# Thirteen of 31 convolution taps formed by ScalarE, four folding instructions moved earlier, and new interleaving tables for the second layer

## The chip, the cores and the metric

The kernel runs on one core of one Trainium2 chip. The metric is the device time of one execution in microseconds (us), the median of several executions. One core has five engines with a queue each: TensorE (PE, matrix products into the PSUM accumulators; PEld is its weight load), VectorE (DVE), ScalarE (ACT), GpSimd (POOL) and SyncE (SP, transfers only). Instructions of one queue run in order, and queues meet through semaphores.

## The reference

A two-layer trunk over 272 tokens (16 learned ones and 256 frames) of width 1024, float32. Each layer does

```
z = rms(h) @ w_in                       # 1024 -> attention | RWKV | convolution columns
h = h + concat[attention(z), rwkv7(z), conv(z)] @ w_out
h = h + peer(rms(h))                    # product-key experts, 128 x 128 of them
```

The attention has 8 query heads over 2 key/value heads, windows of chunks of 64 tokens, a sink for each head. The RWKV-7 part is a recurrence over tokens in 4 heads of 64. The part that the change is about is the convolution, on 256 channels:

```
u = z[..., :256] * sigmoid(z[..., 256:])
u = depthwise_conv(u, conv_w, 31 taps, causal) + conv_b     # u[t] = sum_k conv_w[k] * u[t - 30 + k]
conv = silu(layernorm(u) * ln_g + ln_b)
```

and the end of the RWKV part, `((y_normalised * gn_g + gn_b) + bonus) * g`, which the kernel computes as `y_normalised * (gn_g * g) + (bonus + gn_b) * g`.

## The kernel before, in words

Everything is written out by hand, one program for each engine, with semaphores between them. Data lie with the channels on the 128 partitions and the tokens along the free axis, so a 256-channel array is two halves (j = 0, 1) of 128 x 272.

A layer has these stages. (1) The projection with w_in, 18 weight tiles of 128 x 1024 from memory; ScalarE rounds each tile to w_hi (`high`, L691), GpSimd forms the rest w_lo = w - w_hi (`low`, L609), and TensorE makes three products for each chunk of 128. The input is split likewise into x_hi and x_lo; these two arrays ("projection input fields") are free once the projection is over. (2) The mixers. (3) The projection with w_out, 8 tiles, of the same kind. (4) A norm and the PEER experts, most of the layer's time.

In the mixer stage the recurrence is solved in chunks of 64 tokens, five chunks. VectorE forms decayed arrays (up to L1630, `rh`), TensorE makes the products `gram`, VectorE masks them (L1637), and a triangular inverse is built by doubling in `LEVELS`: in each level b = 0..4 and for each half j, TensorE makes a product, ScalarE copies it out of PSUM (`xm`, L866), TensorE makes two more, VectorE subtracts them (L1664, L1667). `cms` (L1493) prepares the next level's mask. Then come products W and U (copied by L871 on ScalarE and by L1676 on VectorE), the steps from chunk to chunk (`carry`, L1683, L1689, L1694), the output yT (L878), the group norm (L1704 to L1711) and its end (L1717, L1718), which uses `gg` and `bonus`. These two were prepared at L1671 and L1673, two instructions for each half, that stand between the last level and L1676; they are called the folding.

Two other strands are laid between these instructions. The attention runs for each group of query tokens through: scores on TensorE, their combination with the distance (L1523, VectorE), maximum and subtraction (L1529 to L1533), exponentials (L763, L768, ScalarE), normalising (L1541 to L1543), transposes on TensorE (L1059) with copies (L778), outputs on TensorE with a copy (L783). At its beginning the queries' and keys' norms are made: ScalarE's square root (L666, which needs a load of its function table), then VectorE L1501 to L1509, then the first scores. Layer 0 has more groups (the 16 learned tokens too). The convolution's own norm (`conv_norm`: L1552 to L1567 on VectorE, a root and a sigmoid on ScalarE at L666 and L797) is the last strand.

Each engine has a `Beside` that decides where the strands' pieces go: the main sequence calls it at numbered points, and tables give the point for each piece (`ATT_PE`, `ATT_ACT`, `ATT_DVE`, `CONV_...`, one row for each layer). A smaller number is an earlier place in the engine's queue.

The convolution itself runs on GpSimd alone, from the end of its part of the projection. It forms u (L621) with 30 zero columns ahead of it, and then for each of 31 taps k: two TENSOR_SCALAR instructions (L625, one for each half, u shifted by k times the weight column, into `ctmp`) and one TENSOR_TENSOR (L633, `cacc = cacc + ctmp`; none for k = 0). Behind the last tap come the first `low` instructions of w_out (three before they must wait), then the rest of them. What waits for the convolution is the product of its sums on TensorE, near the end of the mixer stage.

## Time and profile before

| | |
|---|---|
| time, median of 3 executions | 2044.98 us (2039.74 to 2053.9) |
| the profiled execution | 2045.54 us |
| its span, first to last instruction | 2043.7 us |
| TensorE busy in the span | 1957.8 us (96%) |
| VectorE busy | 1451.6 us (71%) |
| GpSimd busy | 1222.8 us (60%) |
| ScalarE busy | 969.3 us (47%) |
| mixer stage of layer 0 | about 80 to 193.6 us of the span |
| mixer stage of layer 1 | about 1107.5 to 1215.2 us |

In the rows below a timeline row is: start, duration, engine, line of the source, operation, out<-in with partitions x elements and type, xN for N instructions put together, and in square brackets how long the engine was idle just before and which engine's instruction ended the wait. "arena" is one large array in the core's memory that holds most of the mixers' data; "ps" is PSUM. A windows row gives, for a stretch of the span, the length, the busy time and count of instructions of each engine, TensorE's granted clock as a share of full speed, and the transfers' share and rate. L971 is the helper through which nearly all matrix products go.

### The profile page before, as it was taken

The numbers are of one execution on the slowest core, as the hardware profiler recorded it, in microseconds if no ns is written. First come the engines' busy times: TensorE is split into PE (matmuls) and PEld (weight loads), VectorE is DVE, ScalarE is ACT, GpSimd is POOL, SyncE is SP. The second block draws the span as 40 slices with busy tenths as digits, with TensorE's granted clock in tenths as the row PEclk, the third lists the DMA queues.
The fourth block names the chain that finished last, engine by engine and source line by source line (L and its number), as shares of the span: only waits on it lengthen the run. The fifth ranks groups of instructions, "written<-read, shape, count | busy, mean of one in ns | idle before, by whom it ended". The sixth has DMA issues, their size and how long they took to land.

```text
span 2043.7 us, 43730 instructions
## 1 busy us (share of the span) xinstructions
PE 1957.8 (96%) x16544; PEld 1874.7 (92%) x16544; DVE 1451.6 (71%) x2792; ACT 969.3 (47%) x1663; POOL 1222.8 (60%) x667
## 2 busy tenths in 40 slices
PE   9977999999999999999999879999999999999999
PEld 9866999999999999999989769999999999999998
DVE  3776249975777788788747852599347777887886
ACT  5524455544333455555455234555543334555553
POOL 5893669997666633233048946799966665332330
PEclk9988999999999999999999889999999999999999
DMA  5300445554444599888643004555544446998994
GB/s 197 105 2 18 143 169 194 178 184 156 151 147 144 210 329 315 288 316 310 243 150 124 2 22 154 177 185 195 185 147 152 144 146 246 335 322 302 326 332 149
DMA packets 106382, 388.18 MB, mean 190 GB/s; under 512 B 11808, under 2 KB 12064, under 8 KB 106016
## 3 DMA queue, kind: packets, MB, share of 16 engines
q1 hardware_dynamic: 87840, 319.61, 45.3%
q0 software_dynamic: 18432, 67.12, 9.4%
q8 instruction: 68, 1.11, 0.2%
q14 instruction: 42, 0.34, 0.1%
HBM read 385.63 MB, written 1.05 MB: 189 GB/s over the span
## 4 chain that ended last, share of the span: by engine, by line
PE 61%; POOL 22%; issue 13%; DVE 2%; ACT 1%; DMA 0%; POOLq 0%; ACTq 0%
PE ps L971 61%; POOL w_lo L609 14%; POOL arena L633 4%; POOL arena L625 3%; DMA arena<-ur_c,sel 0%; DVE x L1478 0%; ACT w_hi L691 0%; DVE x_lo L1471 0%; DVE onehots_j L1466 0%; DVE h L1908 0%; POOL arena L621 0%; DVE sel L1794 0%; DVE h L1907 0%; ACT L843 0%; ACT L666 0%
## 5 line engine op out<-in xcount | busy, mean ns | idle before, releaser
L971 PE MATMUL ps<-x_hi,w_hi 128*128 128x240 f32 (+5 forms) x4768 | 1432.2, 324 | 28.9 <-DVE x_lo L1471 12.4
L971 PE MATMUL ps<-x_hi,w_lo 128*128 128x240 f32 (+3 forms) x4768 | 1308.4, 274 | 0.0
L609 POOL TENSOR_TENSOR w_lo<-w,w_hi 128x1024 fp32r<-128x1024 f32 x346 | 869.8, 2531 | 387.1 <-ACT w_hi L691 386.8
L971 PEld LDWEIGHTS ps<-x_hi,w_hi 128*128 128x128 f32 x4768 | 906.3, 190 | 83.9 <-POOL w_lo L609 12.7
L971 PEld LDWEIGHTS ps<-x_hi,w_lo 128*128 128x128 f32 x4768 | 911.1, 191 | 0.0
L691 ACT CAST w_hi<-w 128x1024 fp32r<-128x1024 f32 x596 | 623.9, 1047 | 345.7 <-PE ps L971 177.1
L971 PE MATMUL ps<-x_lo,w_hi 128*128 128x240 f32 (+3 forms) x2720 | 758.6, 279 | 0.0
L971 PEld LDWEIGHTS ps<-x_lo,w_hi 128*128 128x128 f32 x2720 | 520.8, 191 | 0.2
L1865 DVE TENSOR_TENSOR w_lo<-w,w_hi 128x1024 fp32r<-128x1024 f32 x250 | 305.9, 1224 | 113.3 <-ACT w_hi L691 112.6
L971 PE MATMUL ps<-arena 64*64 64x64 f32 (+11 forms) x2580 | 167.4, 266 | 28.0 <-DVE arena L1509 7.9
L971 PEld LDWEIGHTS ps<-arena 64*64 64x64 f32 (+7 forms) x2580 | 146.2, 164 | 48.8 <-issue 16.1
L936 ACT ACTIVATE arena<-ps 128x224 f32<-128x224 f32 (+29 forms) x116 | 31.2, 269 | 264.8 <-PE ps L971 264.8
L918 ACT ACTIVATE arena<-ps 128x240 f32 (+3 forms) x140 | 51.1, 365 | 169.7 <-PE ps L971 169.4
L971 PE MATMUL ps<-onehots_i,onehots_j 128*128 128x128 f32 x928 | 124.0, 277 | 4.8 <-DVE onehots_i L1821 4.8
L971 PEld LDWEIGHTS ps<-onehots_i,onehots_j 128*128 128x128 f32 x928 | 113.5, 193 | 5.2 <-DVE onehots_i L1821 5.2
L644 POOL DMA_INDIRECT x<-v_c,sel x27 | 44.3, 1642 | 102.3 <-DVE arena L1890 56.3
L1830 DVE TENSOR_TENSOR arena<-arena,ps 128x4 f32<-128x4 f32 (+56 forms) x114 | 31.4, 276 | 99.6 <-ACT ps L938 99.6
L1859 DVE TENSOR_TENSOR x_hi<-arena,x_hi 128x240 fp32r<-128x240 f32 (+1 forms) x256 | 100.6, 394 | 0.9 <-ACT x_hi L945 0.9
L945 ACT CAST x_hi<-arena 128x240 fp32r (+3 forms) x256 | 96.9, 380 | 2.4 <-DVE arena L1840 2.4
L1749 DVE MAX8 arena<-arena 128x8 f32<-128x128 f32 (+1 forms) x102 | 25.2, 321 | 96.7 <-ACT arena L908 96.4
L633 POOL TENSOR_TENSOR arena<-arena 128x544 f32<-128x544 f32 x60 | 81.3, 1355 | 5.0
L1814 DVE TENSOR_TENSOR ps<-ps,sel 128x512 f32<-128x512 f32 x116 | 80.1, 691 | 0.0
(198 smaller groups left out, 1655.0 us busy)
## 6 DMA issues: line engine op xcount, KB each, us to landing
w<-u_c SPq DMA_DIRECT2D x256, 512.0 KB, 3.3
w<-v_c SPq DMA_DIRECT2D x256, 512.0 KB, 5.1
w<-w_c SPq DMA_DIRECT2D x84, 512.0 KB, 3.3
arena<-keys_c SPq DMA_DIRECT2D x2, 1024.0 KB, 5.8
arena<-mix_c SPq DMA_DIRECT2D x2, 964.0 KB, 8.4
h<-h SPq DMA_DIRECT2D x2, 544.0 KB, 4.4
out<-x SPq DMA_DIRECT2D x4, 256.0 KB, 2.2
arena<-lora_c SPq DMA_DIRECT2D x2, 256.0 KB, 9.2
```

The costliest lines, as they stand in the source:

```text
L609: g.tensor_tensor(low_of(l, n, wlo_t), low_of(l, n, wraw_t), high_of(l, n).bitcast(F32), ALU.subtract).then_inc(s_lo, 1)
L625: ins = g.tensor_scalar(dst[:, j, :], cu[:, j, k:k + T], vcol(l, "conv_w", j * CONV_K + k), vcol(l, "conv_b", j) if k == 0 else 0.0, ALU.m ...
L633: ins = g.tensor_tensor(cacc[:, :, :], cacc[:, :, :], ctmp[:, :, :], ALU.add)
L644: g.indirect_dma_start(rows[n % ROWS], None, tables[k // SLOTS], bass.IndirectOffsetOnAxis(g_idx[:, k % SLOTS:k % SLOTS + 1], 0)).then_inc ...
L691: nc.scalar.copy(high_of(l, n), low_of(l, n, wraw_t)).then_inc(s_hi, 1)
L918: nc.scalar.activation(hid[l][:, bass.ds(UN * it + i, 1), :].squeeze(1), ps[:, 1 + i % UB, 0:L.nd], ACT.Gelu_apprx_tanh).then_inc(s_gelu, 1)
L945: nc.scalar.copy(act_pair(L, i)[0], hid[l][:, bass.ds(UN * it + i, 1), :].squeeze(1)).then_inc(s_ah, 1)
L971: return nc.tensor.matmul(out_, lhsT, rhs, start=start, stop=stop, skip_group_check=True)
L1814: v.tensor_tensor(eq, iota_ps, bc(sel[:, 1, g:g + OHT], 2, P), ALU.is_equal).then_inc(s_dl, 1)
L1830: v.tensor_tensor(row, row, ps[:, 1 + (L.split + k) % UB, 0:OHT * k], ALU.mult).then_inc(s_hm, 1)
L1859: v.tensor_tensor(al_, hid[l][:, i, :], ah.bitcast(F32), ALU.subtract).then_inc(s_act, 1)
L1865: v.tensor_tensor(low_of(l, n, wlo_t), low_of(l, n, wraw_t), high_of(l, n).bitcast(F32), ALU.subtract).then_inc(s_lv, 1)
```

## The change

Three things.

1. The taps k = 5, 7, 9, ... 27 and 28, thirteen of them, are formed by ScalarE: two ACTIVATE instructions each (Identity with the weight column as scale; `conv_taps`, L828 of the new code), into eight slots of two halves, four in the memory of x_hi (called `taps`) and four in that of x_lo (`x`). GpSimd only adds such a tap (L640 of the new code) after a wait for it. The other 18 taps stay as they were. From the ninth on, ScalarE waits until GpSimd has added the tap whose slot it takes. The instruction that writes x_hi for w_out waits for the whole convolution.
2. The folding stands right behind `rh`, ahead of the masks.
3. The tables of layer 1 are new, for TensorE, ScalarE and VectorE; those of layer 0 are as before, but for `TAP_ACT`, which is new and serves both layers.

```diff
 CONV_PE = ((51, 52,),
-           (51, 52,))
+           (49, 52,))
 CONV_DVE = ((37, 38, 38, 38,),
-            (37, 38, 38, 38,))
+            (36, 38, 38, 38,))
-          (6, 7, 10, 29, 31, 33, 40, 42, 42, 47, 49, 50, 53,))
+          (6, 7, 9, 18, 19, 20, 27, 29, 35, 48, 51, 53, 53,))
+ACT_TAPS = tuple(range(5, 31, 2))[:-1] + (28,)
+TAP_ACT = (0,) * 7 + (1, 1, 2, 2, 3, 4)
+TAP_SLOTS = 8
...
                 for k in range(CONV_K):
+                    if k in ACT_TAPS:
+                        made += 1
+                        pool.wait_ge(s_tap, len(ACT_TAPS) * l + made)
+                        ins = g.tensor_tensor(cacc[:, :, :], cacc[:, :, :], tap(made - 1), ALU.add)
+                        ins.then_inc(s_tapc, 1)
+                        pool.wait_ge(s_tapc, len(ACT_TAPS) * l + made)
+                        continue
...
+            def conv_taps(l):
+
+                act.wait_ge(s_cu, l + 1)
+                for i, k in enumerate(ACT_TAPS):
+                    if i >= TAP_SLOTS:
+                        act.wait_ge(s_tapc, len(ACT_TAPS) * l + i - TAP_SLOTS + 1)
+                    for j in range(2):
+                        ins = nc.scalar.activation(tap(i)[:, j, :], cu[:, j, k:k + T], ACT.Identity,
+                                                   scale=vcol(l, "conv_w", j * CONV_K + k))
+                    ins.then_inc(s_tap, 1)
+                    yield
...
-                beside = Beside((conv_norm(l), CONV_ACT[l]), (attention(l), ATT_ACT[l]))
+                beside = Beside((conv_taps(l), TAP_ACT), (conv_norm(l), CONV_ACT[l]), (attention(l), ATT_ACT[l]))
...
                 act.wait_ge(s_toc, A0[l + 1])
+                act.wait_ge(s_conv, l + 1)
                 x_high(l, 1, cat, L.t0, range(4))
...
                 ask_pe(v.tensor_tensor(rh[:, :, w], dall[:, :, w], r_, ALU.mult))
+                for j in range(2):
+                    link(v.scalar_tensor_tensor(bonus[:, j, :], bonus[:, j, :], vcol(l, "gn_b", j), gg[:, j, :],
+                                                ALU.add, ALU.mult))
+                    link(v.tensor_scalar(gg[:, j, :], gg[:, j, :], vcol(l, "gn_g", j), None, ALU.mult))
...
-                for j in range(2):
-                    link(v.scalar_tensor_tensor(bonus[:, j, :], bonus[:, j, :], vcol(l, "gn_b", j), gg[:, j, :],
-                                                ALU.add, ALU.mult))
-                    link(v.tensor_scalar(gg[:, j, :], gg[:, j, :], vcol(l, "gn_g", j), None, ALU.mult))
                 k, (c0, cn, bank) = [(k, x) for k, x in enumerate(WU) if x[2] == WU_DVE][0]
```

ScalarE's queue in layer 0, from the last copies of the projection's output over the five `vkb` copies to the square root of the attention's norms, before:

```order
L733 COPY arena<-ps 128x272
L853 COPY arena<-ps 128x512 x5
L666 ACT_TABLE_LOAD
L666 ACTIVATE arena<-ps,res 128x272
L666 ACTIVATE arena<-ps,res 128x24
```

and in the changed kernel, whose line numbers are larger by about 21 to 34:

```order
L754 COPY arena<-ps 128x272
L886 COPY arena<-ps 128x512 x5
L828 ACTIVATE taps<-arena,vecs 128x272 x8
L828 ACTIVATE x<-arena,vecs 128x272 x6
L687 ACT_TABLE_LOAD
L687 ACTIVATE arena<-ps,res 128x272
L687 ACTIVATE arena<-ps,res 128x24
```

Seven of the thirteen taps stand between the copies and the table load of the root; the place is the same in layer 1. The other six follow between the copies of the first levels. In layer 1 these places of ScalarE's queue are, before, from the two copies ahead of the levels (L857, L859):

```order
L857 COPY arena<-ps 128x4x128
L859 COPY arena<-ps 128x128
L866 COPY arena<-ps 128x320 x4
L763 ACT_TABLE_LOAD
L763 ACTIVATE arena<-arena 128x144 x4
L768 ACTIVATE arena<-arena 128x4
L866 COPY arena<-ps 128x320 x2
```

and now, where L899 is the copy of a level (`xm`), L828 a tap's half and L784 the exponentials:

```order
L892 COPY arena<-ps 128x128
L899 COPY arena<-ps 128x320
L828 ACTIVATE x<-arena,vecs 128x272 x2
L828 ACTIVATE taps<-arena,vecs 128x272 x2
L899 COPY arena<-ps 128x320
L828 ACTIVATE taps<-arena,vecs 128x272 x4
L784 ACT_TABLE_LOAD
L784 ACTIVATE arena<-arena 128x144 x4
L789 ACTIVATE arena<-arena 128x4
L784 ACTIVATE arena<-arena 128x144 x2
L899 COPY arena<-ps 128x320
L828 ACTIVATE taps<-arena,vecs 128x272 x2
```

Before, the four copies of levels 0 and 1 had nothing between them; now a table load, six exponentials and eight halves of taps stand among the first three of them, and two more halves behind the third.

VectorE's queue in layer 1, at the end of the levels, before (L1523 is the last attention group's scores, L1671 and L1673 the folding, L1683 the first carry):

```order
L1667 TENSOR_TENSOR arena<-arena,ps 128x320
L1541 TENSOR_TENSOR arena<-arena 128x4
L1542 RECIPROCAL arena<-arena 128x4
L1543 TENSOR_TENSOR arena<-arena 128x576
L1671 SCALAR_TENSOR_TENSOR arena<-arena,vecs 128x272
L1673 TENSOR_SCALAR arena<-arena,vecs 128x272
...
L1676 TENSOR_SCALAR arena<-ps 128x512
L1523 SCALAR_TENSOR_TENSOR arena<-arena,ps 128x208 x4
L1529 TENSOR_REDUCE arena<-arena 128x4
...
L1543 TENSOR_TENSOR arena<-arena 128x832
L1683 TENSOR_TENSOR arena<-ps,arena 128x128
```

and now (L1557 scores, L1705 the last updates, L1563 to L1577 the attention's chain, L1710 the copy, L1717 the carry):

```order
L1705 TENSOR_TENSOR arena<-arena,ps 128x320
L1557 SCALAR_TENSOR_TENSOR arena<-arena,ps 128x208 x4
L1705 TENSOR_TENSOR arena<-arena,ps 128x320 x2
L1563 TENSOR_REDUCE arena<-arena 128x4
...
L1577 TENSOR_TENSOR arena<-arena 128x832
L1710 TENSOR_SCALAR arena<-ps 128x512
L1717 TENSOR_TENSOR arena<-ps,arena 128x128
L1723 TENSOR_TENSOR arena<-ps,arena 128x384
```

The last group's scores moved ahead of the last two updates, and the folding is gone from here; nothing of the attention stands between the copy L1710 and the first carry any more.

## Rows read from the trace of the kernel before

**Rows 1.** The page's engine totals, then busy time by stretch (columns as explained above).
```profile
PE 1957.8 (96%) x16544; PEld 1874.7 (92%) x16544; DVE 1451.6 (71%) x2792; ACT 969.3 (47%) x1663; POOL 1222.8 (60%) x667
...
80.00:193.60 113.60, 85.66 (x1419) 74.60 (x1419) 81.06 (x151) 39.77 (x114) 79.30 (x91) 0.84 0.02 6
...
1107.50:1215.20 107.70, 82.82 (x1380) 71.67 (x1379) 69.61 (x127) 35.73 (x93) 78.90 (x91) 0.81 0.02 7
1215.20:1241.00 25.80, 25.74 (x197) 25.23 (x197) 8.62 (x20) 11.51 (x19) 19.84 (x8) 0.92 0.44 144
```

**Rows 2.** Timeline of GpSimd: a tap of layer 0, first w_lo behind it (both layers).
```profile
152.03 0.96 POOL L625 TENSOR_SCALAR arena<-arena,vecs 128x272 f32<-128x272 f32 x2
153.08 1.33 POOL L633 TENSOR_TENSOR arena<-arena 128x544 f32<-128x544 f32 x1
...
156.84 7.73 POOL L609 TENSOR_TENSOR w_lo<-w,w_hi 128x1024 fp32r<-128x1024 f32 x3
...
1184.70 6.97 POOL L609 TENSOR_TENSOR w_lo<-w,w_hi 128x1024 fp32r<-128x1024 f32 x3
```

**Rows 3.** Timeline of ScalarE in layer 0: a scaled pair, the table load, the root.
```profile
41.00 0.98 ACT L828 ACTIVATE arena<-arena,vecs 128x272 f32<-128x272 f32 x2
...
85.55 1.28 ACT L666 ACT_TABLE_LOAD   x1
91.28 0.66 ACT L666 ACTIVATE arena<-ps,res 128x272 f32<-128x272 f32 x2 [4.45 <-PE ps L971]
```

**Rows 4.** Timeline of TensorE: the first scores, behind the root and VectorE's norms.
```profile
97.10 0.39 PE L971 MATMUL ps<-arena 64*16 64x16 f32 x8 [4.11 <-DVE arena L1509]
```

**Rows 5.** Timeline of VectorE in layer 0: mask, attention chain, folding, next scores.
```profile
87.02 0.69 DVE L1637 TENSOR_TENSOR arena<-ps,arena 128x512 f32<-128x512 f32 x1 [9.22 <-PE ps L971]
...
153.66 0.76 DVE L1530 TENSOR_TENSOR arena<-arena 128x4 f32<-128x4 f32 x1
...
155.79 1.71 DVE L1543 TENSOR_TENSOR arena<-arena 128x576 f32<-128x576 f32 x1
157.43 2.58 DVE L1671 SCALAR_TENSOR_TENSOR arena<-arena,vecs 128x272 f32<-128x272 f32 x1
...
165.31 0.69 DVE L1676 TENSOR_SCALAR arena<-ps 128x512 f32<-128x512 f32 x1
167.33 0.90 DVE L1523 SCALAR_TENSOR_TENSOR arena<-arena,ps 128x208 f32<-128x208 f32 x2 [1.33 <-PE ps L971]
```

**Rows 6.** Timeline of TensorE in layer 0 over the same stretch.
```profile
157.65 1.94 PE L1059 MATMUL ps<-res,arena 128*128 128x128 f32 x8 [4.24 <-DVE arena L1543]
159.52 11.88 PE L971 MATMUL ps<-arena 64*64 64x128 f32 x216
```

**Rows 7.** Timeline of VectorE and then of TensorE in layer 1.
```profile
1150.16 0.48 DVE L1667 TENSOR_TENSOR arena<-arena,ps 128x320 f32<-128x320 f32 x1
...
1150.96 0.76 DVE L1543 TENSOR_TENSOR arena<-arena 128x576 f32<-128x576 f32 x1
...
1170.15 0.47 DVE L1667 TENSOR_TENSOR arena<-arena,ps 128x320 f32<-128x320 f32 x1
...
1186.23 1.83 DVE L1523 SCALAR_TENSOR_TENSOR arena<-arena,ps 128x208 f32<-128x208 f32 x4 [8.60 <-PE ps L971]
...
1189.42 2.28 DVE L1531 TENSOR_TENSOR arena<-arena,vecs 128x4 f32<-128x4 f32 x1
...
1193.36 0.28 DVE L1683 TENSOR_TENSOR arena<-ps,arena 128x128 f32<-128x128 f32 x1
...
1201.21 0.92 DVE L1704 SCALAR_TENSOR_TENSOR arena<-ps,arena 128x272 f32<-128x272 f32 x2 [2.48 <-PE ps L971]
...
1179.09 3.23 PE L971 MATMUL ps<-arena 128*64 128x128 f32 x16 [1.41 <-ACT arena L778]
1183.09 9.15 PE L971 MATMUL ps<-arena 64*128 64x208 f32 x176 [0.76 <-ACT arena L783]
...
1215.17 0.55 PE L971 MATMUL ps<-x_hi,w_hi 128*128 128x256 f32 x1 [4.60 <-DVE x_lo L1471]
```

More of the change, by code:

```diff
@@ L94 @@
 CONV_DVE = ((37, 38, 38, 38,),
-            (37, 38, 38, 38,))
+            (36, 38, 38, 38,))
 ATT_PE = ((6, 7, 9, 16, 17, 18, 25, 26, 27, 33, 35, 38, 40, 42, 43, 47, 49, 50, 53,),
-          (6, 7, 10, 29, 31, 33, 40, 42, 42, 47, 49, 50, 53,))
+          (6, 7, 9, 18, 19, 20, 27, 29, 35, 48, 51, 53, 53,))
 ATT_ACT = ((0, 0, 0, 2, 2, 2, 3, 5, 6, 6, 6, 8, 8, 8, 9, 10, 12, 12, 12, 13, 13, 13, 13, 16, 18,),
-           (0, 4, 4, 6, 8, 8, 8, 12, 12, 13, 13, 13, 13, 14, 14, 16, 18,))
+           (0, 2, 2, 2, 3, 4, 4, 6, 6, 6, 8, 10, 13, 13, 16, 18, 18,))
 ATT_DVE = ((0, 0, 1, 2, 6, 8, 8, 13, 15, 15, 21, 21, 21, 30, 31, 31, 32, 32, 32, 34,),
-           (0, 0, 2, 2, 7, 12, 16, 26, 29, 31, 32, 32, 32, 34,))
+           (0, 0, 2, 2, 4, 8, 10, 15, 16, 16, 26, 31, 31, 33,))
 class Layer:
@@ L260, in trunk @@
         h_t = sb("h", DC * T)
-        xh_t = sb("x_hi", DC * T, F32R)
+        xr_t, xh_t = twice("taps", "x_hi", DC * T)
         xn_t, xl_t = twice("x", "x_lo", DC * T)
@@ L275, in trunk @@
         tok = lambda t: t[:, :].rearrange("p (c t) -> p c t", c=DC)
-        xn, xh, xl = tok(xn_t), tok(xh_t), tok(xl_t)
+        xn, xh, xl, xr = tok(xn_t), tok(xh_t), tok(xl_t), tok(xr_t)
         vecs = vec_t[:, :].rearrange("p (l n) -> p l n", l=DEPTH)
@@ L300, in trunk, with tap @@
         tables = ur_c, v_c.rearrange("l i p d -> (l i p) d")
+        def tap(i):
+            c = i % TAP_SLOTS * 2
+            return (xr if c < DC else xn)[:, c % DC:c % DC + 2, :]
         def res(name):
@@ L493, in trunk @@
         s_conv = sem("conv_done")
+        s_cu = sem("conv_input_ready")
+        s_tap = sem("conv_tap_ready")
+        s_tapc = sem("conv_tap_added")
         s_cm = sem("conv_sums_in_psum")
@@ L620, in _ @@
                 link(g.memset(cu[:, :, 0:CPAD], 0.0))
-                link(g.tensor_tensor(cu[:, :, CPAD:CPAD + T], z[:, ZCU:ZCU + 2, 1:T + 1], cacc[:, :, :], ALU.mult))
+                g.tensor_tensor(cu[:, :, CPAD:CPAD + T], z[:, ZCU:ZCU + 2, 1:T + 1], cacc[:, :, :],
+                                ALU.mult).then_inc(s_cu, 1)
+                pool.wait_ge(s_cu, l + 1)
+                made = 0
                 for k in range(CONV_K):
+                    if k in ACT_TAPS:
[5 more added lines that the diff above has]
+                        continue
                     for j in range(2):
```

## The prediction

> **What bounds the kernel now.** I read the page's engine totals first. TensorE is busy in 1957.8 of 2043.7 us, VectorE in 71%, GpSimd in 60%, ScalarE in 47% [rows 1]. TensorE is thus the bound nearly everywhere, and there is only 2043.7 − 1957.8 = 86 us in which it stands still. The busy time by stretch says where: 113.6 − 85.7 = 27.9 us in the mixer stage of layer 0 and 107.7 − 82.8 = 24.9 us in that of layer 1, 53 of the 86 [rows 1]. Behind layer 1's mixers TensorE is busy for 25.74 of 25.80 us. The change touches only the two mixer stages, and in them it adds no matrix product and removes none, so what it can change is these 53 us of waiting and the time in which TensorE runs at less than full clock: the granted share is 0.84 and 0.81 there and still 0.92 in the 25.8 us behind [rows 1].
>
> Then the timelines, one engine after another. A tap takes GpSimd 1.05 us from its first TENSOR_SCALAR to the add and 1.33 + 0.1 for the add, 2.48 in all [rows 2]. The last tap ends at 156.8 and 1184.7, where the first three w_lo begin, while the projection with w_out begins at 193.6 and 1215.2. So the convolution isn't late: the group norm's L1704 starts only at 1201.2 [rows 7], and the product of the convolution's sums stands beside it in the program. GpSimd is a bound of nothing here, and **a shorter convolution gives nothing by itself**. What it can give is less interference: VectorE's instructions with two inputs in the core's memory take longer beside GpSimd. One on 128x4 elements took 2.28 us in layer 1 [rows 7] and another 0.76 in layer 0 and the folding's first 2.58 [rows 5].
>
> **The change part by part.**
>
> *Taps on GpSimd.* Thirteen taps lose their pair: 13 x 1.05 = 13.6 us for each layer. The convolution ends at about 144 and 1172, and the three w_lo of 7.0 to 7.7 us [rows 2] begin there. This costs or gives TensorE nothing directly.
>
> *Denser adds.* The two-input adds now follow each other closer: two in 1.05 + 1.43 + 1.43 = 3.9 us in place of 4.96 in the stretch with alternate taps. If each VectorE instruction with two inputs has to wait for a running GpSimd instruction to end, its mean wait with the old pattern is (2 x 0.48² + 1.33²)/2/2.48 = 0.45 us and with the new (2 x 0.48² + 2 x 1.33²)/2/3.9 = 0.51, an eighth more. There are some ten such instructions on the path up to the levels, so +0.5 to +1.0 us for each layer.
>
> *Seven taps ahead of the root.* This is the part on the path. Their 14 instructions stand between the last `vkb` copy, which ends at 85.5 (the table load begins at 85.55), and the table load of 1.28 us. The same form, 128x272 with a column for scale, took 0.98 us for two, with about 0.41 us from one to the next [rows 3]. So 14 x 0.415 + 0.15 = 5.96 us: ScalarE is through at 91.4 or 91.5, the load ends at 92.7, and the root starts there, where it started at 91.28. The 4.45 us of idle time ahead of the root [rows 3] cover the rest. Delay: **+1.44 us in each layer**. It isn't hidden by what follows: VectorE makes the keys behind the root, and TensorE waited 4.11 us for their last copy, L1509 [rows 4]. The ends for the range: 0 if the pitch is 0.31 us (14 x 0.1 us less), +2.7 if each tap's half takes 0.5 us.
>
> The trace shows no engine idle behind a table load: the next instruction starts at once where its input is there. The Trainium skill, ScalarE: Activation LUTs, "What ACT_TABLE_LOAD costs", has a drain of 1.38 us besides the 1.28 us of each switch; by it the root would be later by 2.8 us and not 1.44 in each layer, and the gain below smaller by 2.8 us in sum. Rows here can't show it, because this root waited anyway.
>
> *The other six taps.* They stand between the level copies. In layer 0 the copies wait for TensorE longer than a tap's 0.83 us, so 0. In layer 1 see below.
>
> *The folding.* In layer 0 it ran from 157.43 to 165.3 on VectorE, 7.9 us, but TensorE had 11.88 us of products from 159.5 on [rows 6], and the next scores then still waited 1.33 us for TensorE [rows 5]. Taking it away there gives 0. At its new place VectorE was idle for 9.22 us ahead of the mask [rows 5]; even with the 7.9 us that they took they fit: 0. Layer 1's queue is the same up to there, so 0 too.
>
> *Layer 0 in sum.* +1.44 for the root, +0.5 for denser adds. Against it stands one gain: the attention chain from 153.66 to 157.5 that TensorE waited 4.24 us for [rows 6] falls behind the end of the convolution, yet beside the w_lo instructions only until about 152. Its normalising took 1.71 us [rows 5] where one of the same shape took 0.76 in layer 1 [rows 7]; that is 0.95, and the first 128x4 instruction with 0.76 us and those behind it hold about as much again, so −2.0 us. **Layer 0: 0 us**, ends −2 and +3.
>
> *Layer 1's tables.* Before, VectorE's last update ended at 1170.6 (call this T) and the first carry started at 1193.36, 22.7 us later [rows 7]. Between them lay the folding, the outputs of one group on TensorE (3.23 us at 1179.09), the scores of the last (from 1183.09; VectorE waited 8.60 us for them) and the whole chain of that group on VectorE, 7.1 us from 1186.23 to 1193.36 with one instruction of 2.28. Now nothing of that stands there but one chain and its normalising (about 5 us), the copy L1710, and TensorE's products U and those for the first state (about 6 after its start): I put 7.0 us from T to the carry. That is **−15.7 us**. The 7.0 is the least sure term of the two: 9.15 us of products followed the last scores' start before [rows 7], scores included.
>
> The same work hasn't vanished; it now stands in the levels. T itself moves: +1.44 from the root, +1.0 for the adds and for the first scores ahead of the levels' start, so +2.4 there. In the second level ScalarE has a table load of 1.28 us, six exponentials of about half a microsecond each (my estimate from the 0.49 us of a tap's half, for fewer elements and a sum) and two taps ahead of the third copy, where before nothing stood between the copies of both levels. These exponentials also wait for VectorE's chain. TensorE has outputs of 3.2 us and scores of 3.1 us (1183.09 to 1186.2) in that level. Following each queue with the durations of the rows, the last update of level b = 1, which ended at 1150.6, ends at 1161.9: +11.3. The later levels have less beside them and win back 1.8: **T +9.5 us**. From carry to L1704 there were 7.85 us [rows 7]; now the second group's normalising, 1 us, can stand in it: +0.9. From there to the first product of w_out, 1215.17, about as before; the root there has a table load behind the last copies, +0.
>
> **Layer 1: −15.7 + 9.5 + 0.9 = −5.3 us**, with about 4 us either way for T.
>
> Sum: 0 − 5.3 = −5.3 us. Against the profiled execution of 2045.54 that is 2040.2, against the median of 2044.98, 2039.7. The three executions of before span 14 us, so the profiled one stands at the median, and I take **2039.5 us**. A change under 1%, 20 us, is about what a measurement of this kernel can't tell from none.
>
> **The rivals.**
>
> *A, the forecast: −2 to −9.* For it: the 22.7 us stretch after T is plainly made of things that aren't needed for the carry, and T's cover is partly idle time.
>
> *B, larger: −9 to −18.* The levels are less delayed than I followed, because TensorE's waits there (24.9 us in the stage) take up the outputs and scores. At T +3 in place of +9.5 it is −12, 2033. Against it: VectorE and ScalarE work in turns there, and a chain on them can't be spread.
>
> *C, the other side: no gain or slower, 0 to +10.* One mechanism: level copies of layer 1 queue behind exponentials and taps that wait for something else, so T moves more. From T +14.8 on nothing is left, since 15.7 − 0.9 = 14.8; at T +20 it is +5, 2050. For it: ScalarE's queue is in order and a tap from the ninth on waits for GpSimd's adds, which pass it only at about 110 in layer 0 and 1137 in layer 1, near the time of that copy.
>
> *D, clock.* TensorE's granted share was 0.92 over 25.8 us behind the stage [rows 1], that is 2 us lost. Another pattern of waiting can move this by ±3 us in a layer. It widens the range on both sides.
>
> *E, the w_lo instructions collide.* They now run at 1172 to 1180, where layer 1's last chain begins. Three VectorE instructions could each be held as L1531 was, for 2.28 us, some 2.1 of it waiting: up to +6 us, and the gain is gone, 2045. Before, that chain was held once as well.
>
> **How the numbers follow.** A 0.50, B 0.18, C with E 0.27, the rest 0.05. The range goes from B's −12 with the clock's −5 to C's +5: 2028 to 2050. Faster by over 1% needs B beyond −20: 0.03. Slower by over 1% needs C at T +35, where more than one copy is stuck: 0.03. Within 1%: 0.94.
>
> **What would show it.** Roots at 92.7 in layer 0, 1.4 later; GpSimd's last add at about 144 and 1172; folding ahead of the first mask with the mask's start unchanged; layer 0's w_out at 193.6 ± 2; in layer 1, T near 1180, first carry at 1187, w_out at 1210 (all against a start of 1107.5). If T is past 1185, C is right; if before 1175, B. The prediction is wrong if the parts outside the mixers move at all, since nothing there was changed.

## The result and the profile after

The changed kernel takes 2054.8 us (median of 22 executions, 2047.2 to 2056.1), the kernel before 2044.0 us (22 executions): the ratio is 1.004, with a 95% interval of 1.0029 to 1.0051. It is slower by 6 to 10 us, where I had forecast 5 us less, and it lies above the range of 2028 to 2050. The ratio is not the quotient of the medians, which is 1.0053: the executions of each kernel fall into two groups (before, 17 of 22 at 2040 to 2046 and 5 at 2049 to 2054; now, 16 at 2053 to 2056 and 6 at 2047 to 2050): a median moves more than the whole does when the larger group changes.

The profiled execution has a span of 2053.4 us, 9.7 more than the kernel before had in its own. The busy time by stretch, of the changed kernel, for the two mixer stages (columns as in [rows 1]):

```profile
80.81:199.75 118.94, 88.50 (x1420) 76.63 (x1419) 75.36 (x147) 50.54 (x140) 62.06 (x65) 0.81 0.02 6
...
1113.84:1226.09 112.25, 82.21 (x1380) 70.81 (x1379) 69.07 (x123) 44.82 (x115) 63.47 (x65) 0.80 0.02 6
```

GpSimd has 17 us less to do in layer 0 and 15 in layer 1, ScalarE 11 and 9 more, and both stages are longer. From the first product of `gram` to the first of w_out, layer 0 takes 118.9 us for 113.6 and layer 1 112.2 for 107.6. Between and behind the mixers the two traces differ by 0.2 and −1.2 us. So the loss is in both mixer stages, half in each, and also in layer 0, whose tables weren't touched. (`gram` starts at 80.81 and 1113.84 now, 0.79 and 6.3 us later than before; I take these off below.)

First the root. Timeline of ScalarE (two rows of layer 1) and of TensorE (layer 0's first scores), changed kernel:

```profile
1125.15 1.28 ACT L687 ACT_TABLE_LOAD   x1
1126.45 0.66 ACT L687 ACTIVATE arena<-ps,res 128x272 f32<-128x272 f32 x2
...
99.54 0.39 PE L1005 MATMUL ps<-arena 64*16 64x16 f32 x8 [4.26 <-DVE arena L1543]
```

The root starts as soon as its table is there, 1.3 us later than before once the offset is off, and the first scores 1.65 us later (99.54 − 97.10 − 0.79, [rows 4]).

Then the place where TensorE's waiting grows most in layer 0. Timeline of VectorE in the attention chain of the fourth level, of GpSimd and of TensorE, and last the same row of TensorE in the kernel before:

```profile
142.41 2.12 DVE L1564 TENSOR_TENSOR arena<-arena 128x4 f32<-128x4 f32 x1
144.56 2.26 DVE L1565 TENSOR_TENSOR arena<-arena,vecs 128x4 f32<-128x4 f32 x1
146.86 0.17 DVE L1566 TENSOR_SCALAR arena<-arena 128x4 f32<-128x4 f32 x1
...
139.85 6.96 POOL L620 TENSOR_TENSOR w_lo<-w,w_hi 128x1024 fp32r<-128x1024 f32 x3
...
148.45 0.87 PE L1093 MATMUL ps<-res,arena 128*128 128x128 f32 x3 [4.66 <-DVE arena L1577]
...
141.84 1.06 PE L1059 MATMUL ps<-res,arena 128*128 128x128 f32 x8 [0.50 <-DVE arena L1543]
```

The convolution ends at 139.85 now, not at 156.84 [rows 2], and the three w_lo of 2.3 us each begin there. Two instructions on 4 elements a partition take 2.12 and 2.26 us, each as long as one w_lo. TensorE waits 4.66 us behind them, and waited 0.50 before.

In layer 1 the same three w_lo meet the masks of a level. Timeline of GpSimd, VectorE, TensorE and ScalarE:

```profile
1173.27 7.97 POOL L620 TENSOR_TENSOR w_lo<-w,w_hi 128x1024 fp32r<-128x1024 f32 x3
...
1173.85 5.18 DVE L1527 TENSOR_TENSOR arena<-arena 128x320 f32<-128x320 f32 x2
...
1188.31 0.49 DVE L1702 TENSOR_TENSOR arena<-arena,ps 128x320 f32<-128x320 f32 x1 [5.70 <-PE ps L1005]
...
1195.85 0.88 DVE L1705 TENSOR_TENSOR arena<-arena,ps 128x320 f32<-128x320 f32 x2
...
1201.41 0.29 DVE L1717 TENSOR_TENSOR arena<-ps,arena 128x128 f32<-128x128 f32 x1 [1.01 <-PE ps L1005]
...
1220.75 3.67 PE L1005 MATMUL ps<-arena 128*64 128x128 f32 x16 [3.50 <-ACT arena L799]
1226.09 0.55 PE L1005 MATMUL ps<-x_hi,w_hi 128*128 128x256 f32 x1 [1.66 <-DVE x_lo L1505]
...
1224.46 0.58 ACT L804 COPY arena<-ps 64x512 f32<-64x512 f32 x1 [3.76 <-PE ps L1005]
```

Two masks take 5.18 us. The last update ends at 1196.7 (the prediction's T, before 1170.6), the first carry starts at 1201.41, and at the end the last attention group's outputs run alone, from 1220.75 to their copy at 1225.0, before x_hi can be made.

To explain this I had one theory and three rivals. **Theory C**, collision (near rival E of the prediction, and not its rival C): a shorter convolution starts the w_lo instructions 17 us earlier, and there they hold VectorE's chains of small instructions. The **rivals**: the root's delay and the denser work, layer 1's tables, or TensorE's clock.

### The profile page after: what moved, and what is told of

The parts are those of the page before. It is cut to its first block, busy times and chain, and to the rows that moved or that the text cites. A ratio compares the mean times of both kernels' runs of the same rounds, so it can differ in the third digit from the quotient of the medians.

```text
span 2053.4 us, 43756 instructions
## 1 busy us (share of the span) xinstructions
PE 1960.8 (95%) x16544; PEld 1877.0 (91%) x16544; DVE 1449.0 (71%) x2792; ACT 990.3 (48%) x1715; POOL 1195.5 (58%) x615
## 4 chain that ended last, share of the span: by engine, by line
PE 63%; POOL 18%; issue 15%; DVE 2%; ACT 1%; POOLq 0%; ACTq 0%
PE ps L1005 63%; POOL w_lo L620 14%; POOL arena L654 2%; POOL arena L646 1%; POOL arena L640 1%; DVE x L1512 0%; DVE x_lo L1505 0%; ACT taps L828 0%; DVE onehots_j L1500 0%; DVE h L1942 0%; ACT x L828 0%; ACT w_hi L712 0%; DVE sel L1828 0%; DVE h L1941 0%; ACT L687 0%
## 5 line engine op out<-in xcount | busy, mean ns | idle before, releaser
L1899 DVE TENSOR_TENSOR w_lo<-w,w_hi 128x1024 fp32r<-128x1024 f32 x250 | 305.7, 1223 | 112.8 <-ACT w_hi L712 112.2
L1005 PE MATMUL ps<-arena 64*64 64x64 f32 (+10 forms) x2580 | 169.0, 267 | 39.7 <-DVE arena L1527 10.9
L1005 PEld LDWEIGHTS ps<-arena 64*64 64x64 f32 (+6 forms) x2580 | 147.2, 164 | 61.5 <-issue 14.0
L1005 PE MATMUL ps<-onehots_i,onehots_j 128*128 128x128 f32 x928 | 123.4, 276 | 4.8 <-DVE onehots_i L1855 4.8
L1855 DVE TENSOR_TENSOR onehots_i<-ps,sel 128x512 f32<-128x512 f32 x116 | 79.3, 684 | 0.3
```

Of the source, the lines that this page charges most:

```text
L1005: return nc.tensor.matmul(out_, lhsT, rhs, start=start, stop=stop, skip_group_check=True)
L1855: v.tensor_tensor(ohA[:, k % 2], eq, bc(sel[:, 0, g:g + OHT], 2, P), ALU.mult).then_inc(s_oh, 1)
L1899: v.tensor_tensor(low_of(l, n, wlo_t), low_of(l, n, wraw_t), high_of(l, n).bitcast(F32), ALU.subtract).then_inc(s_lv, 1)
```

## Experiments: which of the three parts

**Taps alone.** Folding and tables back as they were:

```
-ATT_PE[1], ATT_ACT[1], ATT_DVE[1], CONV_PE[1], CONV_DVE[1]: new
+as in the kernel before; the four folding instructions behind the levels again
```

> Only the thirteen taps go to ScalarE; folding and layer 1's tables as before. Theory C (collision): the first three w_lo instructions of the projection with w_out start 11 to 17 us earlier and stand beside a chain of small VectorE instructions with two inputs in the core's memory; in layer 0 that chain is the same as in the changed kernel, so layer 0's stage is 5 us longer than before, with 1.3 us of it from the root's delay, 2.4 us from denser adds and 3 to 4 us from the collision, less what the chain at 153 us wins. In sum 2044 + 5 for layer 0 + 2 to 4 for layer 1: 2051 to 2053. Rival (tables): the loss comes from layer 1's tables; then the taps alone cost at most the roots' 2.7 us: 2046 to 2047.

Measured: 2053.8 us (2049.5 to 2058.4), ratio to before 1.0029 (1.0009 to 1.0049). Its profiled stages are 120.2 and 111.5 us. This one part has the whole loss, as far as the intervals tell. VectorE and GpSimd in layer 0, in its trace:

```profile
139.54 2.30 DVE L1564 TENSOR_TENSOR arena<-arena 128x4 f32<-128x4 f32 x1
141.88 2.27 DVE L1565 TENSOR_TENSOR arena<-arena,vecs 128x4 f32<-128x4 f32 x1
144.18 2.27 DVE L1566 TENSOR_SCALAR arena<-arena 128x4 f32<-128x4 f32 x1
...
139.47 6.96 POOL L620 TENSOR_TENSOR w_lo<-w,w_hi 128x1024 fp32r<-128x1024 f32 x3
```

Three instructions in a row, 6.8 us for what takes 0.5 us alone: each waits for one w_lo to end.

**Folding alone.**

```
                 ask_pe(v.tensor_tensor(rh[:, :, w], dall[:, :, w], r_, ALU.mult))
+                (the four folding instructions, taken from behind the levels)
```

> Only the folding moves ahead of the masks; all taps on GpSimd, tables as before. Both theories: its new place has 9.2 us of idle VectorE before the mask, its old one was hidden behind TensorE, so 0 in layer 0 (mask of chunk 0 at 87.0 as before) and 0 to -2 in layer 1: 2042 to 2044, ratio 0.999 to 1.000.

Measured: 2045.0 us, ratio 1.0004 (0.9986 to 1.0023). No effect, as forecast.

**Layer 1's tables alone.**

```
-          (6, 7, 10, 29, 31, 33, 40, 42, 42, 47, 49, 50, 53,))
+          (6, 7, 9, 18, 19, 20, 27, 29, 35, 48, 51, 53, 53,))
... (and ATT_ACT, ATT_DVE, CONV_PE, CONV_DVE of layer 1)
```

> Only layer 1's tables are the new ones; all taps on GpSimd, folding where it was. Layer 0 must be as before (113.6 us). Theory C: the tables by themselves are worth about nothing to -5 in layer 1, because the attention's work lies in the levels instead of behind them and the last group's outputs stand alone at the end: 2040 to 2045. Rival (tables): the new tables are the loss of layer 1, +4 to +6: 2048 to 2050.

Measured: 2046.3 us, ratio 1.0005 (0.9991 to 1.0019): nothing that can be measured, and 1.3 us above what theory C gave. Its trace shows why there is no gain. Timeline of VectorE and TensorE in layer 1 (`gram` starts at 1105.88 here, 1.67 us earlier than before):

```profile
1183.91 2.46 DVE L1671 SCALAR_TENSOR_TENSOR arena<-arena,vecs 128x272 f32<-128x272 f32 x1
1186.40 2.32 DVE L1673 TENSOR_SCALAR arena<-arena,vecs 128x272 f32<-128x272 f32 x1
...
1190.67 0.29 DVE L1683 TENSOR_TENSOR arena<-ps,arena 128x128 f32<-128x128 f32 x1 [1.22 <-PE ps L971]
...
1215.94 2.44 DVE L1471 TENSOR_TENSOR x_lo<-arena,x_hi 128x256 fp32r<-128x256 f32 x7 [3.43 <-ACT x_hi L698]
...
1216.51 0.55 PE L971 MATMUL ps<-x_hi,w_hi 128*128 128x256 f32 x1 [1.66 <-DVE x_lo L1471]
```

The first carry is 84.8 us behind `gram`, before 85.8 [rows 7]: the levels took back nearly all that the stretch behind them gave. Part of it is again a collision: the folding still stands behind the levels here, its last two instructions fall on the w_lo, and they take 2.46 and 2.32 us where they took 0.68 and 0.48 before. TensorE stood 7.85 us behind them, so up to 3.6 us of the tables' gain went there. And VectorE then waits 3.43 us for x_hi, which waits for the last group's outputs. That wait is new, and it is the tables' own cost: from L1704 to the first product of w_out it takes 15.4 us, before 14.0.

The layer-0 stage of this kernel, whose code and tables there are those of the kernel before, took 110.7 us in its trace and 113.6 in that of before. A stage of one execution is thus known only to 3 us or worse (another case below has 123.4 us), and the verdicts above go by the times of all executions.

## Experiments: what in the taps costs it

**The root's delay alone.** ScalarE forms the seven taps ahead of the root, nobody reads them, GpSimd's queue is that of before:

```
-                    if k in ACT_TAPS:
+                    if False:
-TAP_ACT = (0,) * 7 + (1, 1, 2, 2, 3, 4)
+TAP_ACT = (0,) * 7          # and only ACT_TAPS[:7] are formed
```

> The kernel before with only the ScalarE work ahead of the root: seven taps are formed there in both layers, and nothing reads them; GpSimd still forms all 31 itself, so its instructions and the place of the first w_lo are unchanged. It measures the root's delay alone. The prediction's term: +1.4 us in each layer, root at 92.7 for 91.3, in sum 2044.7 + 2.8 = 2047.5. Theory C (collision is the larger part): the same. Rival (the delay is the whole loss of the taps, because everything behind the root slips and loses its cover): +8 to +9, 2053.

Measured: 2044.9 us against 2045.05 for before in the same runs, ratio 1.0003 (0.9985 to 1.0022). In the trace the delay is there (VectorE's L1534 waits for the root until 93.00, 13.4 us behind `gram` where it was 11.95, and the first scores stand at 98.18 − 79.62 = 18.6 us for 17.1). In the time, nothing can be seen; the 2.8 us of my sum are inside the interval, 8 to 9 us are not. So the delay isn't the loss.

**The w_lo held back until the chunk steps.**

```
+                pool.wait_ge(s_g, l + 1)
                 lows(l, NZ, NP)
```

> The changed kernel with one wait more: GpSimd starts the first w_lo of w_out only when the products of the chunk steps are in PSUM (about 180 us in layer 0), so that no w_lo stands beside the attention chain or the level masks. Theory C: VectorE's L1564 and L1565 in layer 0 fall from 2.1 and 2.3 us to below 0.3 and 0.3 us, the two masks of 5.18 us in layer 1 to about 1.2; layer 0's stage 3.5 to 4 us shorter than in the changed kernel, layer 1's up to 4: 2054 - 7 = 2047 (2046 to 2050). Rival (root delay and denser adds, or TensorE's clock): the collision isn't on the path, and the time stays at 2053 to 2055.

Measured: 2053.2 us, ratio 1.0036 (1.0019 to 1.0052), where the theory gave 2046 to 2050: as if nothing had been done. By the number alone the collision would have fallen. The trace says otherwise; timeline of VectorE, GpSimd and TensorE in layer 0:

```profile
142.31 0.16 DVE L1565 TENSOR_TENSOR arena<-arena 128x4 f32<-128x4 f32 x1
142.50 0.17 DVE L1566 TENSOR_TENSOR arena<-arena,vecs 128x4 f32<-128x4 f32 x1
...
168.34 6.95 POOL L620 TENSOR_TENSOR w_lo<-w,w_hi 128x1024 fp32r<-128x1024 f32 x3 [28.56 <-PE ps L1006]
...
169.25 1.46 DVE L1565 TENSOR_TENSOR arena<-arena 128x4 f32<-128x4 f32 x1
170.75 2.26 DVE L1566 TENSOR_TENSOR arena<-arena,vecs 128x4 f32<-128x4 f32 x1
173.04 2.27 DVE L1567 TENSOR_SCALAR arena<-arena 128x4 f32<-128x4 f32 x1
...
177.00 1.30 PE L1094 MATMUL ps<-res,arena 128*128 128x128 f32 x5 [6.59 <-DVE arena L1578]
```

The chain at 142 is free now: 0.16 and 0.17 us for 2.12 and 2.26, and TensorE's transposes start 4.2 us earlier (144.29 for 148.45). But the semaphore that I chose comes at 168.3 and not at 180, and the three w_lo fell on the *next* attention chain: TensorE waits 6.59 us where it waited 1.10. The collision had only been moved.

**The w_lo held back to places without such a chain**, with taps and early folding, old tables:

```
+                if l == 0:
+                    pool.wait_ge(s_tn, A0[1])      # last normalising of the attention
+                else:
+                    pool.wait_ge(s_wud, l + 1)     # VectorE's copy behind the levels
                 lows(l, NZ, NP)
```

> Taps and folding as in the changed kernel, layer 1's tables as before, and the first w_lo of w_out held back to where VectorE runs no chain of small two-input instructions: behind the last normalising in layer 0 (about 175 us), behind L1676's copy in layer 1. Theory C: no VectorE instruction beside a w_lo is on the path any more; layer 0's stage falls from 119 to 120 to 113 to 115 us, layer 1's from 111.5 to about 108: 2053.8 - 9 = 2045 (2043 to 2048). Rival (root delay, denser adds and taps in ScalarE's queue carry the loss): 2051 to 2054.

and its control without the wait:

> Taps on ScalarE and the folding early, layer 1's tables as before, and the w_lo instructions right behind the last tap. It is e7_placed without the two waits, so the difference of the two is the collision alone. Theory C: 2052 to 2054, 10 to 11 above e7_placed. Rival (e7_placed owes its time to the folding's new place together with the taps): 2043 to 2046.

Measured: 2042.3 us (2040.7 to 2049.1) with the waits, ratio to before 0.9982 (0.9966 to 0.9998); 2053.8 us (2049.2 to 2056.2) without them, ratio 1.0034 (1.0011 to 1.0057). The medians differ by 11.5 us for two waits on GpSimd, where nobody was in a hurry. The two kernels were not run together; by the ratios, each to the kernel before in its own runs, it is some 11 us as well (1.0034 and 0.9982), as much as the change lost. Timeline of VectorE in layer 0 and 1 and of GpSimd, with the waits:

```profile
142.60 0.16 DVE L1568 TENSOR_TENSOR arena<-arena 128x4 f32<-128x4 f32 x1
...
1179.87 0.16 DVE L1569 TENSOR_TENSOR arena<-arena,vecs 128x4 f32<-128x4 f32 x1
...
183.35 6.96 POOL L620 TENSOR_TENSOR w_lo<-w,w_hi 128x1024 fp32r<-128x1024 f32 x3 [44.32 <-DVE arena L1581]
...
1185.11 6.94 POOL L620 TENSOR_TENSOR w_lo<-w,w_hi 128x1024 fp32r<-128x1024 f32 x3 [6.83 <-DVE arena L1714]
```

Layer 1's stage in this trace is 102.3 us, the shortest of any kernel that computes the convolution (107.6 before, 111.7 in the control). But TensorE stands still in it as long as in the control, 26.6 and 26.2 us; what is shorter is its busy time for the same products (75.7 for 85.5 us), at a granted clock of 0.90 for 0.80. Layer 0's can't be read from it: the profiled execution was the slowest of its ten (2049.1), with TensorE's granted clock at 0.75 in that stage, where [rows 1] has 0.84. Nor is VectorE quite free there. The w_lo now meet an instruction of the group norm, for which TensorE waits 2.47 us and waited 0.85 before:

```profile
188.55 2.34 DVE L1744 TENSOR_TENSOR arena<-arena 128x544 f32<-128x544 f32 x1
```

**The collision without the taps.** This is the strongest test of the place: the kernel before, ScalarE untouched, all taps on GpSimd, and only the three w_lo moved forward.

```
                 for k in range(CONV_K):
+                    if k == (23 if l == 0 else 25):
+                        lows(l, NZ, NZ + 3)
...
-                lows(l, NZ, NP)
+                lows(l, NZ + 3, NP)
```

> The kernel before, all 31 taps on GpSimd and ScalarE's queue untouched; only the first three w_lo of w_out are moved from behind the last tap to ahead of tap 23 in layer 0 (about 137 us) and tap 25 in layer 1 (about 1170 us). The same work in the same queues, at the place where the changed kernel has it. Theory C: VectorE's chain of 128x4 instructions at 137.8 in layer 0 takes some 4 to 6 us longer, in layer 1 2 to 4: 2045 + 8 = 2053 (2050 to 2055). Rival (the loss needs ScalarE's part or the denser adds): 2045, as before.

Measured: 2054.6 us (2054.2 to 2055.4, four executions; before 2043.1), ratio 1.0052 (1.0032 to 1.0073). The loss of the whole change is reproduced by the place of three instructions whose work is the same. (The taps from the 23rd and 25th on, which they pass, run later for it.) Timeline of GpSimd, VectorE and TensorE in layer 0:

```profile
136.75 7.47 POOL L609 TENSOR_TENSOR w_lo<-w,w_hi 128x1024 fp32r<-128x1024 f32 x3
...
136.81 2.31 DVE L1543 TENSOR_TENSOR arena<-arena 128x4 f32<-128x4 f32 x1
139.16 0.18 DVE L1544 RECIPROCAL arena<-arena 128x4 f32<-128x4 f32 x1
139.37 2.65 DVE L1545 TENSOR_TENSOR arena<-arena 128x576 f32<-128x576 f32 x1
141.94 3.33 DVE L1495 TENSOR_TENSOR arena<-arena 128x320 f32<-128x320 f32 x2
...
142.16 1.94 PE L1061 MATMUL ps<-res,arena 128*128 128x128 f32 x8 [5.71 <-DVE arena L1545]
```

**What the collision costs: waits and clock.** The held chain is only the beginning. TensorE's time from these transposes to the next group's, the same 161 products, in the kernel before and then in e10_lows_early:

```profile
141.84:157.65 15.81, 10.70 (x161) 1.00 0.01 2
...
142.16:165.15 22.99, 17.27 (x161) 0.57 0.01 2
```

After the stop of 5.71 us the granted clock was 0.57 over this stretch, mostly the lower of the two levels, 1.2 GHz, where before it was 1.00. Of the 7.2 us that the stretch is longer, 6.6 are slower products. The same split for both stages of the profiled executions, in us (still is the stage less TensorE's busy time; the products are the same in all rows):

| | layer 0: still, busy, clock | layer 1: still, busy, clock |
|---|---|---|
| before | 28.0, 85.6, 0.84 | 24.9, 82.7, 0.81 |
| changed kernel | 30.4, 88.5, 0.81 | 30.0, 82.2, 0.80 |
| e10_lows_early | 29.7, 91.1, 0.79 | 25.2, 85.6, 0.78 |
| e4_taps_fold | 30.5, 88.4, 0.80 | 26.2, 85.5, 0.80 |
| e7_placed | 28.6, 94.8, 0.75 | 26.6, 75.7, 0.90 |
| e5_after_late | 32.3, 86.5, 0.82 | 30.4, 79.4, 0.84 |

So the loss has two parts. In the changed kernel 7.6 us are waits and 2.3 us a lower clock; in e10_lows_early it is 2.1 and 8.3; in e5_after_late 9.8 us are waits, and the clock gives 2.5 back. The executions outside the profile say the same: the median of their mean granted clock is 0.975 to 0.977 for the kernel before, 0.9735 for the changed one, 0.973 for e4_taps_fold and 0.9715 for e10_lows_early, and 0.977 again for e7_placed. That the place of the w_lo brings on the loss is shown by the times. That it does so through TensorE's stop and then the clock fits e10_lows_early, but isn't shown in general: in e7_placed's trace the clock of layer 0 fell too, to 0.53 from 158.94 to 179.95, with no wait of more than 2.3 us in the 14 us ahead of it.

**The changed kernel complete, w_lo behind the last normalising:** `pool.wait_ge(s_tn, A0[l + 1])` ahead of `lows(l, NZ, NP)`.

> The changed kernel complete with its new tables, the first w_lo behind the last normalising of the attention in both layers. Theory C: layer 0 as in e7_placed; layer 1's masks no longer take 5.18 us, but the w_lo now stand at 1203 to 1210, beside the group norm's two-input instructions, which costs 1 to 3 back, and the last group's outputs stay alone at the end: 2054 - 8 = 2046 (2043 to 2049). Rival (layer 1's tables carry the loss of layer 1): 2049 to 2051.

Measured: 2044.5 us (2041.7 to 2052.2), ratio to before 1.0007 (0.9995 to 1.0019). One wait takes back the 10 us. In its trace the w_lo of layer 1 stand from 1200.9 to 1207.9, and one two-input instruction of the convolution's norm (L1589) takes 2.34 us there, 0.73 undisturbed; the last outputs still end the stage. It is not faster than e7_placed, which has the old tables and the w_lo elsewhere in layer 1: without the collision, too, no gain of the new tables shows.

## Experiments: what the taps are worth

**Without taps, w_lo placed:** folding early, the wait on `s_tn`, all taps on GpSimd.

> No taps on ScalarE; folding early; tables as before; the first w_lo behind the last normalising in both layers. It says whether the taps on ScalarE bring anything once the collision is gone. In the kernel before the w_lo stood beside the folding (hidden) in layer 0 and held one instruction for 2.28 us in layer 1: 2045 - 2 = 2043 (2041 to 2045). If e7_placed (2042.3) isn't faster than this by 1 us or more, the thirteen taps by themselves are worth nothing here.

Measured: 2046.7 us (2043.3 to 2058.5), ratio 1.0029 (1.0010 to 1.0049), against the 2043 that I expected: a miss. Its profiled execution (2046.5) has stages of 113.7 and 108.1 us, those of before. One part of the miss can be named: the w_lo hold an instruction of its group norm in both layers, L1707, for 2.33 us each time, where it took 0.73 us before in layer 0. TensorE waits 2.46 us for it in each layer and waited 0.85 before, so 1.6 us each; in layer 1 the chain that [rows 7] shows held for 2.28 us is free in return. The rest stays open: three of the ten executions took 2053.7 us or more, at a mean granted clock of 0.968 in the slowest two. Against it, e7_placed is 4.4 us faster, so the taps on ScalarE may bring something once nothing is in their way, some 2 to 4 us. That isn't shown: the two aren't from the same runs, and the place of the w_lo in layer 1 differs.

**Three taps ahead of the root, eleven in all:**

```
-ACT_TAPS = tuple(range(5, 31, 2))[:-1] + (28,)
-TAP_ACT = (0,) * 7 + (1, 1, 2, 2, 3, 4)
+ACT_TAPS = (5, 7, 9, 15, 17, 19, 21, 23, 25, 27, 28)
+TAP_ACT = (0,) * 3 + (1, 1, 2, 2, 3, 3, 4, 5)
```

> As e7_placed, but only three taps (k = 5, 7, 9) stand ahead of the root, so that 3 x 0.83 + 0.15 + 1.28 = 3.9 us fit into the 4.45 us of idle time there; eleven taps in all (the others k = 15 to 28, between the level copies). Both theories: the root starts at 91.3 + 0.4 again, 1.3 us earlier than in e7_placed in each layer: 2.5 us faster than e7_placed, 2042 to 2043 by theory C, 2049 to 2051 by the rival.

Measured: 2046.8 us (2045.8 to 2050.0), ratio 1.0006 (0.9993 to 1.0020): not 2.5 us faster than e7_placed but 4.5 slower. Timeline of ScalarE, VectorE and TensorE in layer 0:

```profile
91.40 0.66 ACT L691 ACTIVATE arena<-ps,res 128x272 f32<-128x272 f32 x2 [1.97 <-PE ps L1009]
...
96.23 1.45 DVE L1545 SCALAR_TENSOR_TENSOR arena<-arena 128x272 f32<-128x272 f32 x1
...
98.67 0.39 PE L1009 MATMUL ps<-arena 64*16 64x16 f32 x8 [5.56 <-DVE arena L1547]
```

The root is on time again, at 91.4. But VectorE's six instructions behind it now meet GpSimd at another phase, one of them takes 1.45 us for 0.50, and the first scores stand where they stood with seven taps: 18.5 us behind `gram`. A gain of 1.3 us on one engine was lost to interference before it reached TensorE. That explains why it isn't faster than e7_placed; why it is 4.5 us slower stays open.

**GpSimd without 29 of the 31 taps**, to see what all of the interference costs. The kernel leaves these taps out, so its convolution is not the reference's; folding and waits are as in e7_placed:

```
-                for k in range(CONV_K):
+                for k in (0, CONV_K - 1):
```

> GpSimd leaves out 29 of the 31 taps (only the first and the last are computed, so the convolution part of the output isn't the reference's); folding early, tables as before, the w_lo instructions placed as in e7_placed. It measures what all of GpSimd's convolution costs the mixers by interference. If VectorE's waits for GpSimd cost what the rows show (0.45 us for each of about 15 two-input instructions on the path of a layer, and 2 to 4 us where chains stand): each stage 8 to 12 us shorter, 2044.7 - 20 = 2025 (2020 to 2030). If interference is mostly hidden: 2038 to 2043.

Measured: 2018.1 us (2014.4 to 2023.5, four executions), ratio 0.9866 (0.9839 to 0.9893), 2 us below the range that I expected. The busy time by stretch in its trace:

```profile
80.84:180.76 99.92, 82.16 (x1419) 71.00 (x1419) 58.65 (x147) 39.69 (x114) 8.12 (x4) 0.88 0.02 7
...
1094.18:1187.44 93.26, 76.30 (x1380) 66.39 (x1379) 53.19 (x123) 35.58 (x93) 8.09 (x4) 0.89 0.03 8
```

Each stage is 14 us shorter. VectorE's busy time in the first falls from 81.1 [rows 1] to 58.7 us; 7.7 of the 22 are the folding, which now stands ahead of the stage, and the other 15 I read as waiting for GpSimd inside instructions that count as busy. TensorE stands still 18.1 us less in the two stages, and its products take 9.9 us less at the higher clock. GpSimd is the bound of nothing in this kernel, and yet its taps cost 27 us.

## Why the prediction was wrong

*TensorE bounds, and only the mixer stages can change:* right. Outside them the traces differ by 0.2 and 1.2 us.

*GpSimd's savings:* mis-sized. I put the convolution's end 13 us earlier; it is 17.0 earlier in the trace, 17.8 with the offset, in part because the add of a ready tap takes 1.15 us (up to 1.28) and not 1.33. That makes 2.3 of the 4 us; the rest I haven't followed.

*"This costs or gives TensorE nothing directly":* **the step that failed.** I had the three w_lo at 144 and 1172 and looked only at what became free, the chain at 153.7, for which TensorE indeed waits 2.23 us in place of 4.24, as I had worked out. I didn't ask what stood where the w_lo would go. In layer 0 it was the chain ahead of that one: TensorE waited 4.1 us more, and its products up to the next chain took 12.6 us for 10.7, at a granted clock of 0.83 for 1.00. Before, the w_lo had fallen on the folding, [rows 5] with 2.58 us for one instruction, which was hidden: the cover for the w_lo was part of the old order. e10_lows_early and e7_placed show this step from both sides.

*Rival E* was this mechanism, with the right price for an instruction (2.28 us held), but only for layer 1 and only as a way to lose the gain, with C at 0.27 together. In layer 0 it had no entry, so the range ended at 2050.

*Rival D*, the clock at ±3 us in a layer, was too small: TensorE's busy time for the same products was 5.5 us longer in layer 0 of e10_lows_early than before, and 9.2 longer in that of e7_placed. And I had it as independent of the waits, while the kernels with the collision in layer 0's fourth level have the lower clock in most executions.

*Seven taps ahead of the root, +1.44:* right, 1.3 us in the trace. Its worth in the time isn't measurable (e6_root_delay). The Trainium skill, ScalarE: Activation LUTs, "What ACT_TABLE_LOAD costs", has a drain of 1.38 us on top of the 1.28 of a switch; the trace doesn't agree: the root starts 0.02 us after its load ended (1125.15 + 1.28, 1126.45), and the delay is 1.3 and not 2.8 us.

*Denser adds, +0.5 to +1.0:* 0.9 us from the first scores to the first level's products in this trace, but not settled. That stretch of layer 0 takes 10.6 to 12.6 us in the six traces with all taps on GpSimd and 11.3 to 13.5 in the seven with taps on ScalarE.

*Folding:* right in both. VectorE's idle time ahead of the mask went from 9.22 [rows 5] to 7.15 us.

*Layer 1's tables, −15.7 + 9.5 + 0.9:* the second step that failed, mis-sized above all in T. T moved by 19.8 us and not 9.5, so by the prediction's own sign its rival C came true in this layer (the masks of 5.18 us are 3.3 of that; in the level behind them VectorE waits 5.70 us for TensorE, which works on outputs and scores), and from T to the carry it is 4.7 us and not 7.0. The carry stands 1.75 us later, not 6.2 earlier. From the carry to L1704 it is +1.4 and not +0.9. Left out: the last group's outputs at the end of the stage. From L1704 to the first product of w_out I had "about as before"; it is +1.5 us (15.4 for 14.0), and e3_tables has the same 15.4.

## What to carry to other kernels

When an edit shortens a queue that isn't the bound, list what comes forward in that queue and put each piece beside what stands at its new time on the other engines. Work with slack belongs behind a wait on an event, not right behind whatever came before it: the two waits on GpSimd turned +10 us into −3. Beside GpSimd a short VectorE instruction pays up to the whole length of its long neighbour, so a chain of 0.16 us instructions is the worst place for it; and when such a wait shows no gain, look in the trace where the piece went before giving up the theory. And split a stage into TensorE's standing still and its busy time before adding up waits: here a stop of 5.7 us was followed by 6.6 us of slower products.

## What the runs showed of the hardware

A VectorE instruction on 128x4 elements, 0.16 us alone, takes 2.1 to 2.3 us beside w_lo instructions of 2.3 us, and several in a row each wait for one. The Trainium skill, SBUF — State Buffer, "Who interferes with whom", has a VectorE instruction with two inputs in the core's memory contend with a GpSimd instruction that reads there, and calls it an exclusive lock; the trace agrees, one w_lo for each. I hadn't expected that a TENSOR_SCALAR with one input in the core's memory, 128x4 (L1566 of e1_taps above, 2.27 us), is held just as long. Instructions that read one input from PSUM weren't lengthened (the changed kernel's L1702 at 1179.06, beside a w_lo, 0.49 us). ScalarE's fourteen tap halves took 5.88 us beside GpSimd, a steady 0.41 us from one to the next.

The clock moved much between executions of one code. The same block of 216 products, 11.88 us in [rows 6], took 19.21 us in the trace of e7_placed, with a granted share of 0.53 from 158.94 to 179.95; there, most of the block ran at the lower of the two levels, 1.2 GHz.

```profile
160.81 19.21 PE L1009 MATMUL ps<-arena 64*64 64x128 f32 x216
```
